# Where ScalarE takes the first residual's root in a slot: ahead of the slot's exponentials and norm, or behind them

## What is computed

```python
h = x * (1.0 + scale1) + shift1
z = h @ w_in
a_out = chunk_sgu(gelu(ua), gelu(va), w_s, b_s)          # mixer A
b_out = mla_attention(q_nope, q_rope, k_nope, keys_kr, v) # mixer B: 4 heads, softmax over the keys
mix = jnp.concatenate([a_out, b_out], axis=-1) @ w_o
x = layer_norm(ALPHA * x + gate1 * mix, ln1_g, ln1_b)     # the first residual
h2 = x * (1.0 + scale2) + shift2
x = layer_norm(ALPHA * x + gate2 * peer(h2, ...), ln2_g, ln2_b)
```

## Time and profile before

| | |
|---|---|
| median of 3 runs | 3303.42 us (3303.32 to 3306.32) |
| the profiled execution | 3311.13 us, of which the span of the trace 3309.3 us |
| TensorE busy | 3210.9 us (97% of the span) |
| VectorE busy | 2597.5 us (78%) |
| ScalarE busy | 1239.1 us (37%) |
| GpSimd busy | 1573.6 us (48%) |
| stage `middle` | about 340 to 1139 us of the span |

### The profile page before, as it was taken

The page is one execution under the profiler, slowest core; times in us unless marked ns, Lnnn a source line. Parts: engine busy times, 40 slices in busy tenths (PEclk is TensorE's granted clock), DMA queues, the critical chain, the costliest instruction groups (busy, mean ns, idle before and its releaser), DMA issues.

```text
span 3309.3 us, 46438 instructions
## 1 busy us (share of the span) xinstructions
PE 3210.9 (97%) x17082; PEld 2749.0 (83%) x17082; DVE 2597.5 (78%) x5340; ACT 1239.1 (37%) x2294; POOL 1573.6 (48%) x983
## 2 busy tenths in 40 slices
PE   9999899999988799999999999999999999999996
PEld 4656578887877699899889899999999999999996
DVE  0222358888888789898999888889999998888866
ACT  2232343343335733333343333333343333333333
POOL 1200004788877178788888888223333332222201
PEclk8999999999999999999999999999999999999998
DMA  9701636676766699999999999999899999999943
GB/s 373 292 21 37 264 141 197 192 199 182 201 185 198 260 342 359 333 360 338 352 339 361 354 353 379 367 342 361 341 373 364 350 367 354 352 354 350 353 164 113
DMA packets 291073, 952.93 MB, mean 288 GB/s; under 512 B 93220, under 2 KB 146596, under 8 KB 232103
## 3 DMA queue, kind: packets, MB, share of 16 engines
q1 hardware_dynamic: 154312, 513.35, 42.2%
q0 software_dynamic: 136256, 436.55, 38.1%
q10 hardware_dynamic: 288, 0.16, 0.0%
HBM read 888.71 MB, written 61.24 MB: 287 GB/s over the span
## 4 chain that ended last, share of the span: by engine, by line
PE 43%; DVE 14%; DMA 6%; issue 2%; ACT 1%; SPq 0%; DVEq 0%; ACTq 0%
PE bank L1768 22%; PE bank L1782 21%; DMA work<-in_u 6%; DVE ring L1897 4%; DVE acc L1914 3%; DVE uL L2085 2%; DVE vL L2080 2%; DVE ga L2112 1%; DVE cL L2077 1%; ACT uR L1857 0%; ACT vR L1849 0%; DVE slots L2019 0%; DMA work<-x_scratch 0%; DVE cs L1905 0%; DVE st L2043 0%
## 5 line engine op out<-in xcount | busy, mean ns | idle before, releaser
L1729 POOL DMA_INDIRECT ring<-in_uv,slots x384 | 582.4, 1517 | 798.9 <-DVE carry L1914 681.8
L163 POOL DMA_INDIRECT g_cells<-slots x384 | 705.6, 1837 | 315.3 <-DVE slots L1475 196.9
L1768 PE MATMUL bank<-hR,uR 128*128 128x384 f32 x2048 | 689.4, 337 | 22.3 <-DVE uL L2085 22.3
L1768 PE MATMUL bank<-hR,uL 128*128 128x384 f32 x2048 | 688.5, 336 | 0.0
L1768 PE MATMUL bank<-hL,uR 128*128 128x384 f32 x2048 | 687.1, 335 | 0.0
L1843 ACT ACTIVATE cR<-ga 128x384 fp32r<-128x384 f32 x256 | 134.7, 526 | 963.9 <-PE bank L1782 568.5
L1782 PE MATMUL bank<-vR,cR 128*128 128x512 f32 x1536 | 477.5, 392 | 0.7 <-DVE slots L2019 0.7
L1782 PE MATMUL bank<-vR,cL 128*128 128x512 f32 x1536 | 476.0, 391 | 0.0
L1782 PE MATMUL bank<-vL,cR 128*128 128x512 f32 x1536 | 475.7, 391 | 0.0
L1897 DVE CUSTOM_DVE_ANT_0 ring<-ring,slots 128x1024 f32<-128x1024 f32 x384 | 467.7, 1255 | 0.0
L1768 PEld LDWEIGHTS bank<-hR,uR 128*128 128x128 f32 x2048 | 385.5, 188 | 36.3 <-DVE uL L2085 26.5
(11 more groups left out here) (317 smaller groups left out, 4111.8 us busy)
## 6 DMA issues: line engine op xcount, KB each, us to landing
work<-in_u SPq DMA_DIRECT2D x256, 512.0 KB, 6.5
work<-in_v SPq DMA_DIRECT2D x256, 512.0 KB, 7.0
work<-in_w_pq SPq DMA_DIRECT2D x36, 2048.0 KB
work<-in_w_o SPq DMA_DIRECT2D x18, 2048.0 KB
g_cells<-work POOLq DMA_DIRECT2D x32, 768.0 KB, 7.2
work<-g_blocks SPq DMA_DIRECT2D x32, 768.0 KB, 13.7
work<-g_cells SPq DMA_DIRECT2D x32, 768.0 KB, 8.7
g_blocks<-big SPq DMA_DIRECT2D x8, 2048.0 KB, 6.3
```

Source lines behind the costliest of these rows:

```text
L163: pool.indirect_dma_start(out=cells_of(g_dram, i), out_offset=bass.IndirectOffsetOnAxis(ap=slots[:, i, D + k:D + k + 1].bitcast(U32), axis=0),
L1729: pool.indirect_dma_start(out=ring[:, k % R, :], out_offset=None, in_=a["uv"], in_offset=bass.IndirectOffsetOnAxis(ap=ids[:, k // P, k % P ...
L1768: mm = pe.matmul(A[t][:, 0:CW], w[:, t, k, :], h[:, k, :], start=(k == 0 and w is uR and h is hR), stop=(k == DK - 1 and w is uL))
```

## The change

One call of `root` moves down in ScalarE's order within the same slot. Ahead of the change the order in the slots h = 1 is: `turned(n)`, `root(i - 1)`, `exp(n + 1)`, `norm(n)`, query copy, `high(i + 1)`, `spread`. With it: `turned(n)`, `exp(n + 1)`, `norm(n)`, `root(i - 1)`, query copy, `high(i + 1)`, `spread`. Nothing else is touched: no engine's other work, no buffer and no semaphore.

```diff
                     if h == 0 and 3 <= i < LAST + 2:
                         exps(i - 3)
-                    if h == 1 and 0 <= i - 1 < LAST:
-                        root(i - 1)
                     if h == 2:
...
                         exp(n + 1)
                     if n < NH:
                         norm(n)
+                    if h == 1 and 0 <= i - 1 < LAST:
+                        root(i - 1)
                     for what, ch in EARLY_MOD.get(n, ()):
```

## The result

The changed kernel took 3336.72 us (median of four runs, 3326.67 to 3336.78) against 3303.37 us before. The ratio is 1.0085, with a 95% interval of 1.0072 to 1.0098. In four more runs, made later beside other kernels, it took 3327.08 to 3335.07 us (median 3329.09, ratio 1.0077, interval 1.0060 to 1.0094). All eight together have their middle at 3332.4 us. The change makes the kernel slower by some 23 to 33 us.

A forecast was written before the change was run, and what follows sets the result against it. TensorE, without a gap in the middle stage from its fourth tile, bounds the kernel. Terms 15.5 + 3.7 + 0.7 + 0 = 19.9 us, 28.9 with the clock, gave 3332 us, 0.9% slower; range 3318 to 3338.

The forecast's parts named there:

- Nothing is gained ahead of the exponentials: From the fourth tile on, exponentials wait for nb 0.66 us longer than for the load, so they gain 0.
- VectorE waits 3.68 us: VectorE's reciprocal waits for the root, now behind exponentials and norm; it and the work behind it come 3.68 us later.
- The chain through the rotary copy, 3.1, 3.3, 2.9, 3.4 and 2.8 us: Tile index 3 to 7: late residual delays ScalarE's rotary copy and the copies TensorE's third transposes need; sum 15.5 us.
- The 0.85 us to spare at slot 15: TensorE comes to slot 15 0.85 us after its norm is done; VectorE's 0.6 us of extra lateness fits in.
- Slot 9, nothing: Tile index 2: nb of slot 10 moves 3.68 us, but its norm is done before TensorE asks; cost 0.
- Slot 33, 3.7 us by VectorE alone: Tile index 8: no next rotary part; VectorE's lateness goes on to the next maxima and sums, costing the whole 3.7 us.
- Slot 5, +0.7 us: Tile index 1: norm up to 1.48 us earlier, but a 1.28 us load precedes slot 6's exponentials; 0.6 of gain arrives.
- The clock, 9 us: TensorE's clock falls behind the five stalls and the wait ahead of slot 7, 1.5 us each; lower end 0.
- The switch in its new place: ScalarE's table switch for the root behind the norm takes 1.28 us and nothing beside it; number of loads unchanged.
- The rival of a dearer switch: Table switch straight behind the norm takes as long again: 1.28 x 6 = 7.7 us more, 3340; chance 0.02.
- The loss passes through to the end: The middle stage's loss reaches the kernel's end unchanged, as the last stage starts behind a barrier and keeps its length.
- the terms without the clock: Five stalls 15.5, slot 33 3.7, slot 5 0.7, slot 9 0: 19.9 us in all, giving 3323 us.

The follow-up runs named there:

- first profile: Profiled execution of the changed kernel (root behind the norm) from its first four runs, against the kernel before; it ends at 3335.0 us.
- second profile: Profiled execution of the same changed kernel from the later call, beside other kernels; it ends at 3325.3 us.
- the first experiments: Changed kernel with rotary copy moved to the next slot, 3331.71 us; with half the lists ahead of the residual's output, 3329.35; with both edits, 3308.25.
- the experiment that cut the first chain: Changed kernel with the next tile's rotary copy moved into the next slot, behind the copies TensorE needs: 3331.71 us, ratio 1.0081.
- when VectorE's wait was filled: Changed kernel with the first half of the slot's lists ahead of the residual's output on VectorE: 3329.35 us, ratio 1.0072.

## Why the prediction was right

The forecast was 3332 us, by a loss of 28.9; the measured loss is 33.4 us in the first comparison and 23.4 in the second. In the timelines `middle` loses 27.2 us in the first profile and 23.3 in the second, from the first product with w_o to the next stage.

- *Nothing is gained ahead of the exponentials*: right. In the five tiles they wait for nb, and start with it (5.88 us of idle instead of a load).
- *VectorE waits 3.68 us*: right, 3.71 in the rows above and in all eight slots; 29.9 us in nine waits with one that was there before. The parts that the forecast names add up to 3.64, which changes nothing.
- *The chain through the rotary copy, 3.1, 3.3, 2.9, 3.4 and 2.8 us*: right, 2.89, 2.88, 2.77, 3.24 and 2.38 in the first profile, 14.2 instead of 15.5. Per tile the kernel lost 2.8 to 3.7 us at full clock (second profile), 15.7 in all. That this was the cause and that VectorE's own lateness stood right behind it is shown by the first experiments, each chain cut alone and both together.
- *The 0.85 us to spare at slot 15*: right by the experiment that cut the first chain. With TensorE on time, 2.6 us of wait appeared; what the prediction did not see is that the rotary transposes of line 967 meet VectorE's lateness before line 993 does.
- *Slot 9, nothing*: right, 0.0 in both profiles.
- *Slot 33, 3.7 us by VectorE alone*: 4.2 and 4.4, and 0.2 when VectorE's wait was filled. From the product in slot 32 to the norm of slot 35 it takes 961.22 - 908.87 = 52.35 us, before 936.21 - 887.51 = 48.70: +3.65, the size forecast. The place was only partly right. The profile shows the loss first at slot 35's opening transposes, and it remained. The timelines of TensorE and ScalarE of the changed kernel, then the product in slot 32 of the kernel before:

```profile
908.87 3.60 PE L923 MATMUL bank<-work,slots 128*128 128x512 f32 x8
...
953.95 0.30 PE L993 MATMUL bank<-ident,on 128*128 128x128 f32 x1 [2.93 <-ACT on L1200]
...
962.67 0.66 PE L938 MATMUL bank<-ident,slots 128*128 128x128 f32 x4 [0.25 <-ACT carry L1156]
...
961.22 0.37 ACT L1200 ACTIVATE on<-bank,ri 128x128 f32<-128x128 f32 x1 [3.96 <-DVE ri L1344]
```

```profile
887.51 3.60 PE L923 MATMUL bank<-work,slots 128*128 128x512 f32 x8
```

  The clock fell behind this stall too, to 0.61 and 0.67 in the two profiles (the last window at the end of this text). By the forecast VectorE would cover that; it did not wholly: TensorE's transposes behind that norm began 962.67 - 961.22 = 1.45 us after it, before 937.12 - 936.21 = 0.91, and 1.61 in the second profile. These 0.5 to 0.7 us are the rest of slot 33's loss.

- *Slot 5, +0.7 us*: right in size. From TensorE's norm transpose in slot 5 to the one in slot 7 it took 427.74 - 405.88 = 21.86 us, before 427.76 - 406.70 = 21.06: +0.8 (second run +0.8 as well, 426.46 - 404.61 = 21.85). The load ahead of slot 6's exponentials came where it was expected. That the gain was put at 0.6, between none and 1.48, was a guess, and the agreement to 0.1 us is partly luck: in the first profile TensorE's wait ahead of slot 6 became 1.4 us shorter (2.10 instead of 3.54), a wait of 0.48 at the third group of transposes was added, and the wait ahead of slot 7 became 1.4 us longer (3.58 instead of 2.15). The rest of the 2.4 us measured for this tile, 1.6, is clock: behind the longer wait it was 0.72 over 6 us in both profiles where it had been 1.00, which loses 6.0 x 0.28 = 1.7 us. The timelines of ScalarE and TensorE, slots 5 to 7 of the changed kernel, which answer to the earlier trace rows, and the windows behind the wait, columns as in rows 2:

```profile
424.25 1.28 ACT L1180 ACT_TABLE_LOAD   x1
425.54 0.58 ACT L1180 ACTIVATE pr<-bank,nb 128x384 f32<-128x384 f32 x1
...
405.88 0.27 PE L993 MATMUL bank<-ident,on 128*128 128x128 f32 x1
...
427.74 0.30 PE L993 MATMUL bank<-ident,on 128*128 128x128 f32 x1 [3.58 <-ACT on L1200]
```

```profile
427.70:431.00 3.30, 3.26 (x14) 2.52 (x14) 0.58 (x2) 1.43 (x4) 0.00 (x0) 0.70 0.00 0
427.70:433.70 6.00, 5.96 (x24) 4.54 (x25) 1.48 (x4) 1.44 (x5) 0.00 (x0) 0.72 0.00 0
```

- *The clock, 9 us*: mis-sized, the one term that was. All six places were taken to fall. Of these, four did in the first profile: three stalls, of 1.3 to 1.5 us by the difference of the table's two runs, and slot 7, together 5.7 us. In the second only slot 7 did, 1.6 us. So it is a term of some 2 to 6 us that changes from execution to execution. The price of one fall, 1.5 us, was right, and the number of falls was too high.
- *The switch in its new place*: 1.28 us for the load and 0.02 to the root behind it (557.26 in the rows above), as in slot 5 before. The rival of a dearer switch is out.
- *The loss passes through to the end*: right, by the distances given above; what the last stage adds or takes is its own spread.

So the mechanism held, and so did the terms without the clock: 19.9 us were forecast, and the second profile has 20.1 + 2.4 = 22.5, of which 1.6 is clock in slot 7, so 20.9. The first has 24.0 + 2.4 = 26.4 with 5.7 of clock, so 20.7. The clock was put too high by 3 to 7 us. What the first comparison has beyond the tiles' 26.4 us lies between executions, as the last stage's 2165 to 2170 us do. That the forecast meets the middle of the eight runs to 1 us is therefore partly luck: the clock was too high, and the spread of the rest made it good. The 7.7 us that the median was put under the profiled execution, as before the change, did not come again either: the changed kernel's first four runs have 3336.72 and 3336.78.

## What to carry to other kernels

Moving a short step behind longer work on an engine with much idle time is not free when another engine waits for it in order: the wait is paid there, and it can come back to the first engine through any later copy that needs the result. Ask of each wait that a move makes longer which instructions stand behind it, on both engines, and how many microseconds the fullest engine leaves before it asks for them. In the slots shown here these were 0.7 and 0.85 us, against a wait of 3.7. Where two such chains run side by side, cutting one shows the other; here only both together brought the time back, to 1.0010.

## What the runs showed of the hardware that was not expected

Gaps of the same length do not always bring TensorE's clock down. Behind stalls of 2.77 and 2.38 us it was 0.58 and 0.52 in one execution of the changed kernel, behind stalls of 2.76 and 2.61 it was 1.00 in another, and a stall of 2.89 left it at 1.00 in the first. A gap of 2.10 ahead of slot 6 brought it to 0.68 in the first, while in the kernel before one of 2.15 ahead of slot 7 left it at 1.00. The windows behind the gap of 2.10 and behind the stall of 2.93 in slot 35, changed kernel, first profile, columns as in rows 2:

```profile
414.20:417.50 3.30, 3.27 (x14) 2.56 (x14) 1.71 (x3) 1.40 (x2) 0.00 (x0) 0.68 0.00 0
954.00:957.30 3.30, 2.43 (x14) 2.13 (x15) 3.20 (x21) 2.65 (x6) 0.74 (x1) 0.61 1.13 365
```

A table load of 1.28 us on ScalarE was followed by its function 0.02 us later in every slot where nothing else was awaited.
